# Gates of the merge by seven products of half depth, with weights in chunks of 128 features

## The reference

```python
h = rms_norm(x, norm1_g[l]) * (1.0 + sc1) + sh1
q, k, v, gu, gv, ga, gb = jnp.split(h @ w_in[l], splits, axis=-1)
y_a = sliding_window_attention(q, k, v, positions, sinks[l], rel_bias)
y_b = spatial_gating(jax.nn.gelu(gu), jax.nn.gelu(gv), ...)
merged = jax.nn.sigmoid(ga) * (y_a @ p_a[l]) + jax.nn.sigmoid(gb) * (y_b @ p_b[l])
x = x + g1 * (merged @ w_o[l])
```

## Time and profile before

| | |
|---|---|
| runs, median (lowest to highest) | 2903.73 us (2903.48 to 2909.48) |
| the profiled execution | 2907.39 us, of which the span of the profile 2905.9 |
| PE busy | 2639.3 us, 91% of the span |
| DVE, ACT, POOL busy | 1110.4, 648.2, 372.8 us |
| mean granted clock of PE | 0.96 of full speed |
| the merge, first gate product to first output product | 373.1 to 720.9 us |

### The profile page before, as it was taken

The page is one execution under the profiler, slowest core; times in us unless marked ns, Lnnn a source line. Parts: engine busy times, 40 slices in busy tenths (PEclk is TensorE's granted clock), DMA queues, the critical chain, the costliest instruction groups (busy, mean ns, idle before and its releaser), DMA issues.

```text
span 2905.9 us, 35506 instructions
## 1 busy us (share of the span) xinstructions
PE 2639.3 (91%) x13610; PEld 1302.4 (45%) x13610; DVE 1110.4 (38%) x2785; ACT 648.2 (22%) x1528; POOL 372.8 (13%) x422
## 2 busy tenths in 40 slices
PE   5999999999978999999769998999999599999982
PEld 3466944444443333343334764555545333333431
DVE  3223927555252222221181114777743512212214
ACT  3214710000131111110050002656532111111101
POOL 1000000000001111110122111222520101111002
PEclk9999999999988999999989999999999799999996
DMA  8221005635339998998851111000020499999997
GB/s 308 116 80 59 2 29 174 201 123 190 147 133 415 399 407 345 407 403 313 331 197 57 44 44 30 30 30 16 30 111 29 188 405 374 394 360 387 354 413 288
DMA packets 206672, 607.49 MB, mean 209 GB/s; under 512 B 58593, under 2 KB 114153, under 8 KB 157225
## 3 DMA queue, kind: packets, MB, share of 16 engines
q1 hardware_dynamic: 150248, 540.16, 47.6%
q0 software_dynamic: 56256, 65.07, 6.6%
HBM read 559.22 MB, written 52.18 MB: 210 GB/s over the span
## 4 chain that ended last, share of the span: by engine, by line
PE 82%; DVE 8%; DMA 5%; issue 2%; SPq 1%; ACT 1%; POOL 0%; DVEq 0%; POOLq 0%; ACTq 0%
PE ps L1929 20%; PE ps L1891 10%; PE ps L1056 7%; PE ps L2602 6%; PE ps L1379 4%; PE ps L550 4%; PE ps L1060 4%; PE ps L3102 3%; PE ps L2599 3%; DMA R<-in_w_up 3%; PE ps L556 2%; PE ps L1872 2%; PE ps L2877 2%; PE ps L1861 2%; PE ps L862 1%
## 5 line engine op out<-in xcount | busy, mean ns | idle before, releaser
L1929 PE MATMUL ps<-R 128*64 128x512 f32 (+1 forms) x3496 | 636.8, 523 | 25.1 <-DMA R<-in_w_up 20.0
L1929 PEld LDWEIGHTS ps<-R 128*64 128x64 f32 (+1 forms) x3496 | 205.7, 127 | 310.3 <-issue 278.1
L1891 PE MATMUL ps<-R 128*64 128x512 f32 (+1 forms) x1720 | 284.3, 515 | 1.4 <-DVE R L1752 1.4
L1056 PE MATMUL ps<-R 128*128 128x512 f32 x512 | 225.6, 600 | 5.1 <-DMA R<-in_w_in 4.6
L1829 ACT ACTIVATE R<-ps 64x512 f32<-64x512 f32 (+1 forms) x97 | 52.5, 541 | 615.2 <-PE ps L1929 615.2
L1780 DVE TENSOR_TENSOR R<-ps,R 64x512 f32<-64x512 f32 (+1 forms) x97 | 59.8, 617 | 322.5 <-ACT R L1829 203.5
L1891 PEld LDWEIGHTS ps<-R 128*64 128x64 f32 (+1 forms) x1720 | 97.2, 127 | 171.4 <-issue 156.9
L1056 PEld LDWEIGHTS ps<-R 128*128 128x128 f32 x512 | 97.7, 192 | 128.9 <-issue 122.8
L1752 DVE COPY R<-ps 128x256 f32<-128x256 f32 (+1 forms) x97 | 38.0, 392 | 292.4 <-PE ps L1872 292.4
L1815 ACT ACTIVATE R<-ps,small 128x128 f32<-128x128 f32 (+1 forms) x172 | 64.6, 455 | 359.8 <-PE ps L1861 359.8
L1929 PE MATMUL ps<-XR,R 128*64 128x512 f32 (+1 forms) x376 | 118.0, 509 | 1.6 <-DVE R L1743 1.6
(11 more groups left out here) (374 smaller groups left out, 3927.3 us busy)
## 6 DMA issues: line engine op xcount, KB each, us to landing
R<-in_w_up SPq DMA_DIRECT2D x127, 1024.0 KB, 17.2
R<-in_w_down SPq DMA_DIRECT2D x116, 1024.0 KB, 18.0
R<-in_w_gate SPq DMA_DIRECT2D x107, 1024.0 KB, 18.8
R<-in_w_ada SPq DMA_DIRECT2D x40, 1024.0 KB, 5.5
XR<-in_w_gate SPq DMA_DIRECT2D x21, 1024.0 KB, 20.3
R<-in_w_in SPq DMA_DIRECT2D x7, 2048.0 KB, 13.7
R<-in_w_in SPq DMA_DIRECT2D x13, 1024.0 KB, 5.3
XR<-in_w_down SPq DMA_DIRECT2D x12, 1024.0 KB, 22.8
```

What stands on the lines that cost most here:

```text
L1056: i_ = T.matmul(o, wv[:, kk, cols], k.hT[:, kk, tk], start=kk == 0, stop=kk == 7)
L1891: i_ = T.matmul(k.ps[r * j:r * j + r, 5 + b % 2, 0:n], v.hT[b % 2][:, c:c + r], w[:, kk % 2, n * j:n * j + n], start=kk == 0, stop=kk == 3)
L1929: i_ = T.matmul(hidden_out(k.ps[P0 + r * j:P0 + r * j + r, b % 2, 0:n], r), x_, hidden_columns(w, r, j), start=kk == 0, stop=kk == 7)
```

## The change

Both gates of a chunk of 128 features are taken together. With A11, A12 the two depth halves of ga's weights, A21, A22 those of gb's, and B11, B21 (first tokens) and B12, B22 (last 512 tokens) the depth halves of h, the four outputs (two gates, two halves of the tokens) come from seven products of depth 512 (four matmuls each) of sums of the A's and sums of the B's. The order on PE is 1, 2, 6, 5, 7, 4, 3, and then the branches A0, B0, A1, B1. Products 1, 6, 7 are added up in one bank, and 5 and 3 in another; ACT copies the bank after 1, 6 and 7 (`v.kept`), DVE adds a second bank to a copy for each of the four outputs (`v.sig`), and ACT takes the sigmoid in place. There are now 8 chunks of 11 groups.

The sums of h (t1 to t4, 128x2048 each) are formed once by POOL during the input projection, t3 in place over h. The sums of the weights (s1 to s4, 128x512 each) are formed by POOL per chunk, for chunk c once product 3 of chunk c - 1 is done. Gate weights arrive per chunk, 1 MB in rows of 512 B, in two halves of slot 0; chunk c + 2 is asked for ahead of the quarter of the fourth step of chunk c. STEPS becomes pairs: 2 or so after product 3, four (later three) after the branches. A job's finish waits for the bank it uses alone. w_o is asked for once product 3 of chunk 6 (its first MB) and of chunk 7 (the rest) are done.

```diff
+def gpsimd_token_sums(k):
+    done = s["z_q"]
+    G.wait_ge(s["p_in"].sem, 8)
+    G.tensor_tensor(v.t1, k.hT[:, 0:4, 512:1024], k.hT[:, 0:4, 0:512], ALU.subtract).then_inc(*done.up())
+    G.wait_ge(s["p_in"].sem, 16)
+    G.wait_ge(done.sem, 3)
+    G.tensor_tensor(v.t2, k.hT[:, 4:8, 512:1024], v.t1, ALU.subtract).then_inc(*done.up())
+    G.wait_ge(done.sem, 4)
+    G.tensor_tensor(v.t4, k.hT[:, 4:8, 0:512], v.t2, ALU.subtract).then_inc(*done.up())
+    G.wait_ge(s["p_in"].sem, NF)
+    G.tensor_tensor(v.t3, k.hT[:, 4:8, 512:1024], v.t3, ALU.subtract).then_inc(*done.up())
...
-STEPS = (4, 4, 3, 3, 3, 3, 3, 0, 3, 3, 3, 3, 3, 2, 0, 0)
+STEPS = (2, 4, 2, 4, 2, 4, 2, 4, 2, 4, 2, 3, 2, 3, 0, 0)
...
-    if job:
-        T.wait_ge(s["v_fin"].sem, FIN_V[job - 1])
     if job in ROWS:
         for hf in range(2):
             n = mod_group(job, hf)
+            if n >= 2:
+                T.wait_ge(s["v_fin"].sem, n - 1)
...
-MERGE = [(what, c) for it in range(18) for what, c in (("a", it), ("b", it), ("A", it - 2), ("B", it - 2)) if 0 <= c < 16]
+TURNS1 = "1265743"
+MERGE = [(what, c) for c in range(8) for what in list(TURNS1) + ["A0", "B0", "A1", "B1"]]
...
 def vector_merge(k):
+    for c in range(8):
+        for o, turn, kept in (("11", "2", "1"), ("22", "5", "7"), ("21", "4", "7"), ("12", "3", "6")):
+            V.wait_ge(s["p_mg"].sem, MERGED[turn, c])
+            V.wait_ge(s["a_sig"].sem, SIGNED[kept, c])
+            if c:
+                V.wait_ge(mg.sem, ADDED["m1", c - 1])
+            V.tensor_tensor(v.sig[o], k.ps[:, merge_bank(turn, c), :], v.kept[kept], ALU.add).then_inc(*mg.up())
+        for job in finished_at(2 * c):
+            vector_mod_finish(k, job)
+        for n in steps_of(2 * c):
+            vector_mod_sum(k, n)
+        for hf in range(2):
...
+        for n in steps_of(2 * c + 1):
             vector_mod_sum(k, n)
...
+def gpsimd_merge(k):
+    G.wait_ge(s["a_ya"].sem, 64)
+    for c in range(8):
+        wa, wb = v.w[c % 2][:, 0], v.w[c % 2][:, 1]
+        a11, a12, a21, a22 = wa[:, 0:4], wa[:, 4:8], wb[:, 0:4], wb[:, 4:8]
+        G.wait_ge(s[f"d_w{c % 2}"].sem, 64 + 32 * (c // 2))
+        if c:
+            G.wait_ge(s["p_mg"].sem, MERGED["3", c - 1])
+        G.tensor_tensor(v.s1, a21, a22, ALU.add).then_inc(*gs.up())
+        G.wait_ge(gs.sem, gs.n)
+        G.tensor_tensor(v.s2, v.s1, a11, ALU.subtract).then_inc(*gs.up())
+        G.tensor_tensor(a21, a11, a21, ALU.subtract).then_inc(*gs.up())
+        G.wait_ge(gs.sem, SWEPT + 4 * c + 2)
+        G.tensor_tensor(v.s4, a12, v.s2, ALU.subtract).then_inc(*gs.up())
...
 def tensor_merge(k):
+        if what in ("6", "5", "7", "3"):
+            T.wait_ge(s["g_clr"].sem, SWEPT + 4 * c + {"5": 1, "6": 2, "7": 3, "3": 4}[what])
+        if what in ("6", "7"):
+            T.wait_ge(s["a_sig"].sem, SIGNED["1" if what == "6" else "6", c])
+        elif what == "3":
+            T.wait_ge(s["v_mg"].sem, ADDED["22", c])
...
+            for kk in range(4):
+                i_ = T.matmul(o, left[:, kk, :], right[:, kk, :], start=what in "1254" and kk == 0, stop=kk == 3,
+                              skip_group_check=True)
...
     for n in range(40):
-        if n == sum(STEPS[:5]) + 2:
-            sync_gate_weights(k, 1)
-        if n == sum(STEPS[:7]) + 2:
+        for c in range(6):
+            if n == sum(STEPS[:2 * c]) + 3:
+                sync_gate_weights(k, c + 2)
+        if n == sum(STEPS[:7]) + 3:
             sync_branch_weights(k, 1)
...
 def sync_out_weights(k):
     for h2 in range(2):
-        Q.wait_ge(s["p_mg"].sem, MERGED["ab"[h2], 15])
         for a_ in range(2):
+            Q.wait_ge(s["p_mg"].sem, MERGED["3", 7 if h2 or a_ else 6])
```

More of the change, by code:

```diff
@@ L992, in tensor_mod_finish @@
     else:
+        T.wait_ge(s["v_fin"].sem, mod_group(job, 0) - 1)
         for j in range(4):
@@ L1026, in scalar_merge @@
     v = merge_views(k)
[L1027 to L1033, removed]
+    for c in range(8):
+        for turn in "167":
+            S.wait_ge(s["p_mg"].sem, MERGED[turn, c])
+            if c:
+                S.wait_ge(s["v_mg"].sem, ADDED["12", c - 1])
+            S.copy(v.kept[turn], k.ps[:, merge_bank(turn, c), :]).then_inc(*s["a_sig"].up())
+        for o in ("11", "22", "21", "12"):
+            S.wait_ge(s["v_mg"].sem, ADDED[o, c])
+            S.activation(v.sig[o], v.sig[o], ACT.Sigmoid).then_inc(*s["a_sig"].up())
+def gpsimd_merge(k):
+    G, s = k.nc.gpsimd, k.s
+    v = merge_views(k)
+    gs = s["g_clr"]
+    G.wait_ge(s["a_ya"].sem, 64)
+    for c in range(8):
+        wa, wb = v.w[c % 2][:, 0], v.w[c % 2][:, 1]
+        a11, a12, a21, a22 = wa[:, 0:4], wa[:, 4:8], wb[:, 0:4], wb[:, 4:8]
+        G.wait_ge(s[f"d_w{c % 2}"].sem, 64 + 32 * (c // 2))
+        if c:
+            G.wait_ge(s["p_mg"].sem, MERGED["3", c - 1])
[5 more added lines that the diff above has]
+        G.tensor_tensor(v.s4, a12, v.s2, ALU.subtract).then_inc(*gs.up())
 def tensor_merge(k):
@@ L1039, in tensor_merge @@
     T.wait_ge(s["a_ya"].sem, 64)
[L1040 to L1056, removed]
-        else:
-            w4, x4 = ((v.wa, v.yaT), (v.wb, v.uT))[j - 2]
+    T.wait_ge(s["z_q"].sem, 6)
@@ L1061, in tensor_merge @@
         i_.then_inc(*s["p_mg"].up())
-        if what == "B":
-            for job in finished_at(cnt):
+        if what in ("3", "B1"):
+            for job in finished_at(2 * c + (what == "B1")):
                 tensor_mod_finish(k, job)
@@ L1121, in sync_merge @@
     sync_gate_weights(k, 0)
+    sync_gate_weights(k, 1)
     sync_branch_weights(k, 0)
@@ L1362, in tensor_out @@
     lhsT = merge_views(k).mT
-    T.wait_ge(s["v_mg"].sem, 48)
+    T.wait_ge(s["v_mg"].sem, 80)
     for n in range(17):
@@ L2400 @@
 LN_BEFORE = 4 + 3 * NT
-CLEARED = 56
+CLEARED = 88
 def mixes_of(g):
@@ L3170, in gpsimd_program @@
     gpsimd_zero_rows(k)
+    gpsimd_token_sums(k)
     gpsimd_attn(k)
+    gpsimd_merge(k)
     gpsimd_out_weights(k)
```

89 lines of the change are left out of this document (62 added, 27 removed).

## The result

The changed kernel took 2890.31 us (median of 5 runs, 2886.72 to 2894.33) where the kernel before took 2904.32 (5 runs, 2903.48 to 2909.48): ratio 0.9949, 95% interval 0.9938 to 0.9960, -14.0 us. On another chip it was 2887.01 (2883.30 to 2890.53) against 2903.53 (11 runs, 2898.34 to 2907.29): 0.9948 (0.9935 to 0.9961), -16.5. So it is faster, as forecast, but by about half of the -27 forecast, and 1.3 us above the range. The rival "bigger waits" had said 2889.

A forecast was written before the change was run, and what follows sets the result against it. PE's own instructions were taken to bound the merge. Savings of 29.0 and 7.5 us, less the waits in chunks and ends, gave -27.0: 2880.4 profiled, 2877 as median, range 2866 to 2889.

The forecast's parts named there:

- bigger waits: Rival, chance 0.20: gate chunks at 5.6 us or POOL's 5.1 put product 3 some 2 later in five chunks; 2889.
- gates by seven products: PE in the merge: 28 matmuls per chunk instead of 32, gates from 221.4 to 192.4 us, -29.0.
- no wait for gate weights, no slow clock behind it: PE in the merge: 4.63 us of idling for gate weights and 2.84 of slow clock go, -7.5.
- chunk 1: Product 3 waits for DVE's output 22: 0.8 us for POOL and 0.4 for the loads, +1.2.
- chunk 3, chunk 5: Product 3 waits 0.3 us, and some 0.4 more for the loads, +0.7.
- chunk 4: Branch weights ahead of quarter 23 make output 22 late: PE idles 3.5 us, 2.0 more for the clock, +5.5.
- end of the merge: POOL's multiplication of w_o delays DVE's last sum, +0.7 us (bounds 0 and 4).
- POOL against DVE: First-half modulation steps: turns on SBUF with POOL's four weight sums cost DVE 3.4 us (bounds 0 and 5.1).
- The loads between the quarters: Gate chunk ahead of the fourth step's quarter takes 3.7 us, some 0.4 more wait each in chunks 1, 3, 5.
- The slow clock: Behind PE's idling in chunk 4: 2.0 us, scaled from 2.84 after 4.63.
- The attention's start: POOL's sum t3 holds SBUF until 259.0, where DVE's small operations lie on PE's path: +0.7 us (bounds 0 and 1.5).

The follow-up runs named there:

- the repeat: The changed kernel profiled once more with no edit; merge 327.7 us, against 333.0 in the first trace.
- kernel 8: As 7, with the fourth step of each burst also moved behind output 22; 2873.17 us, ratio 0.9893 to the kernel before.
- 3: Changed kernel with POOL's weight sums over one of 128 columns, the rest left out; merge 324.1 us.
- 4: Changed kernel with only an eighth of each gate load from chunk 2 on; merge 324.2 us.
- 5: Changed kernel with the same bytes of gate weights in rows of 2 KB from chunk 2 on; merge 325.3 us.
- 6: Changed kernel with the second branch load at a quarter of its bytes (0.5 MB instead of 2); merge 323.7 us.
- 10: Changed kernel with the second branch load of p_a over 128 partitions, same number of bytes, other values; merge 330.3 us.
- 7: Changed kernel with branch weights moved ahead of quarter 24, gate chunks ahead of the second quarter behind the burst; 2873.62 us, ratio 0.9895 to the kernel before.

## Why the prediction was wrong in size and right in kind

Step by step, for the merge, in us. "After" is the profiled execution, 332.98 long; the repeat is 327.73 long.

| step | predicted | after | repeat |
|---|---|---|---|
| gates by seven products | -29.0 | -27.3 | -27.3 |
| no wait for gate weights, no slow clock behind it | -7.5 | -7.5 | -7.5 |
| chunk 1 | +1.2 | +6.0 (3.0 idle, 3.0 clock) | +1.9 |
| chunk 3 | +0.7 | +1.0 | +1.0 |
| chunk 4 | +5.5 | +9.9 (7.8 idle, 2.1 clock) | +8.4 (7.0 idle, 1.4 clock) |
| chunk 5 | +0.7 | +1.9 | +1.9 |
| ends of products around the waits | 0 | +1.3 | +1.3 |
| end of the merge | +0.7 | +0.4 | +0.6 |
| sum | -27.7 | -14.3 (measured -14.84) | -19.7 (measured -20.1) |

Chunk 4 costs 2.9 to 4.4 more than predicted in both. Chunk 1 is far off in the first alone, so a part of the miss there is chance.

Three lines of the kernel before, for the price of what is removed: a branch product, a finish, and the branch product behind the gate products of 684.17.

```profile
659.37 3.60 PE L1060 MATMUL ps<-XR,R 128*128 128x512 f32 x8
662.89 0.64 PE L994 MATMUL ps<-R,cst 128*32 128x256 f32 x8
...
697.90 3.60 PE L1060 MATMUL ps<-R 128*128 128x512 f32 x8
```

- **The gates.** Six gate products take 645.25 - 624.55 = 20.70, with 0.1 of the finish ahead of them in it, so 3.43 each, as much as predicted, and the wait for weights is gone. The price taken for what is removed was a little high. I read 6.92 for a gate product from 663.46 to 677.30, but a finish of a column job stood just ahead of it, and its tail was in that record; two gate products with none ahead take 697.90 - 684.17 = 13.73 (684.17 is in the earlier trace rows), 6.865 each. 32 x 6.865 - 192.4 = 27.3. A finish costs 0.76, not 0.57: from 659.37 to 663.46 are 4.09 where a branch product alone takes 3.435, and 0.11 more are in the gate products behind. With these, PE's work in the merge is 192.4 + 109.9 + 7 x 0.76 + 3.5 = 311.1, and kernel 8, which has no wait before a product 3, is busy for 311.20 us. (The 1.3 of the table is what the after-trace is busy beyond this and the slow clock, 317.45 - 311.1 - 5.1. Elsewhere in it the clock is full; a product's record is 3.60 long and the next starts 3.43 behind it, an overlap that is lost at each wait.) That the product chain gives what it says is thus shown.
- **POOL against DVE.** Right: 3.4 was expected, 3.3 came, and with POOL's sums down to one column it is gone (3).
- **The step that failed is "The loads between the quarters".** It treated SP's loads as a row in which each waits for those ahead of it and for nothing behind it, at 2.7 to 3.7 us a MB. Instead a load under way shares the DMA engines with those asked for after it. A quarter asked for 1 us ahead of the gate chunk landed in 7.9 (7.3 to 7.4 in two other traces) instead of the 5.6 to 5.7 it takes with an eighth of the chunk or none behind it, and the one behind in 10.7 (9.5) instead of 5.4 to 5.5. That makes 3.0 in the burst (2.0 in the repeat) where 0.4 was counted (4 removes it; 5 says that 0.4 to 1.9 of it is the row length). The 3.7 us for the MB itself were not too little: 304 to 313 GB/s make 3.4. In chunk 4, quarter 22 is delayed in the same way (step 22 waits 3.33; it takes 7.8 to land, and 6.5 with a quarter of the 2 MB behind it in 6): it lands 3.5 later than predicted. And the 2 MB are slower than the 2.7 us a MB assumed, mostly since p_a goes to 64 partitions at a time (10): from quarter 22 to quarter 23 it is 10.3 (9.5 in the repeat) and not 8.1, so quarter 23 lands 5.7 later than predicted. That it is their place that decides what these bytes cost is shown by 7: with the same bytes the merge is 11 us shorter than in the repeat and 17 shorter than in the first trace of the change.
- **The slow clock** was scaled from one row (2.84 behind 4.63 of idling). Measured as what product 3 takes above 3.67, it is 3.0 behind 3.02, 2.7 behind 3.61, 1.4 behind 3.52, 1.4 behind 6.99, 2.1 behind 7.76 and 2.7 behind 9.15 (and 1.9 to 2.8 behind the other five waits of 5.4 to 8.1 in the table): a price of 1.4 to 3.0 for each idling from 3 us up, not one that grows with it. The 2.0 expected for chunk 4 was right by it. But chunk 1 was given no slow clock, and so a wait that came out 1.8 longer than expected cost 4.8 more.
- **The rival "bigger waits"** had nearly the right sum (2889; 2890.31 was measured) for one partly right reason, which is luck in part. The gate chunks do cost PE more than assumed, though not by taking 5.6 us each. Its other one (POOL at 5.1) isn't there, and it had nothing of its own on chunk 4, where 2.9 (repeat: 6.99 + 1.44 - 5.5) to 4.4 of the loss are.
- **The range** ended at 2889 because the terms of chunk 4 had no upper bound of their own: the price of the 2 MB was taken from a row of loads over 128 partitions, and the slow clock was scaled.
- **The attention's start** was to cost 0.7. From the end of the input projection's last product to the start of the merge it is 118.8 us before and 117.9 (after, repeat) to 119.0 in the others, and the wait for DVE of 261.28 in the earlier trace rows ends 6.9 behind that last product before and after alike. Nothing of that size can be seen.

Open: why the clock falls behind some waits of about 2 us and not behind others. Before the output PE idles 1.92 to 2.23 in eleven traces; in six 15.7 follow (1.7 lost), in five 14.0 to the same product. At product 3, 1.7 follow 2.01 and 2.17 of idling, and nothing follows 2.15. No experiment here separates these.

Open too: why chunk 1's wait varies from 1.86 to 3.61 in kernels that are the same up to there.

## What to carry to other kernels

When an edit moves an in-order engine to within half a microsecond of the critical path, price every load under way in its stretch, those asked for *after* the data it waits for too, and ask at which place in the schedule the consumer has slack; here moving two kinds of load was worth as much again as the change first gave: 2873.62 us against 2903.64 is -30.0, where the change alone gave -14.0 and -16.5. Take a load's rate from a row with the same partitions and row length, since the busy share of the DMA engines reads full in either case. And read an instruction's price from a row with nothing else ahead of it.

## What the runs showed of the hardware

- While two loads to 64 partitions each were under way, among others, 233 GB/s were moved with the DMA engines at a share of 1.04; with the same bytes over 128 partitions it was 349, at 1.02.
- A load of 1 MB asked for 1 us ahead of another MB landed in 7.3 to 7.9 us, and in 5.6 to 5.7 where that other one was small or not there.
- Four POOL sums that read SBUF (1.27 and 1.26 us, the last two 1.45 each) stretch a chain of eight short DVE instructions by 3.3 us in all.
- A wait of PE of 3 us or more cost 1.4 to 3.0 us in slow clock behind it, and its length did not tell which: 3.0 behind 3.02, 1.4 behind 3.52 and 6.99, 2.7 behind 9.15.
